# Prologue tiles taken in pairs, gate rows in four column groups of TensorE, and two products fewer per mLSTM head

## The reference, cut to what matters

```
shift, scale, gate = split(silu(c) @ w_ada + b_ada, 3)          # c (1, 1024), w_ada (1024, 3072)
h    = x * (1 + scale) + shift                                   # x (1024 tokens, 1024)
proj = h @ w_in + b_in        # q,k,v,z of the attention | q,k,v,o,z of the mLSTM | i, f (4 + 4 columns) | merge gates
A: causal stick-breaking attention, 8 heads of 64          -> y_sb
B: mLSTM in chunks, 4 heads of 128, state C, n, m carried  -> y_ml
   per chunk:  num = w_inter * (q @ C) + s_mat @ v ;  den = w_inter * (q . n) + sum(s_mat)
               C   = decay * C + (wk * k)^T @ v ;     n   = decay * n + sum(wk * k)
   init:       C = 0, n = 0
y   = (sigmoid(g_A) * y_sb + sigmoid(g_B) * y_ml) @ w_out
out = LayerNorm(2^0.25 * x + (1 + gate) * y) * ln_g + ln_b
```

## Time and profile before

| | |
|---|---|
| median of three executions | 959.51 us |
| the profiled execution, its own time | 959.67 us |
| its span (first to last instruction) | 957.8 us |
| outside the span | 1.9 us |
| TensorE busy with matmuls | 928.8 us, 97% of the span |
| VectorE, ScalarE, GpSimd busy | 616.0, 441.2, 165.5 us |
| mean granted TensorE clock | 0.997 |

### The profile page before, as it was taken

How to read it: one execution, slowest core, us unless ns; L and a number is a source line. 1 busy time by engine, 2 the same in 40 slices (tenths; PEclk the granted TensorE clock), 3 DMA queues, 4 the chain that set the end, 5 groups by cost and what they waited for, 6 DMA issues and landing times.

```text
span 957.8 us, 12945 instructions
## 1 busy us (share of the span) xinstructions
PE 928.8 (97%) x4989; PEld 760.7 (79%) x4989; DVE 616.0 (64%) x1104; ACT 441.2 (46%) x719; POOL 165.5 (17%) x114
## 2 busy tenths in 40 slices
PE   1999999999999999999999999999999999999996
PEld 1677888888888888888888888888888888887885
DVE  4856886755976647966649867534653333345997
ACT  2454566653675544675445666525743222243100
POOL 1010132220232220322311322201100000002210
PEclk9999999999999999999999999999999999999998
DMA  8942211112201022111112111127612212215232
GB/s 221 291 110 49 66 44 34 34 35 66 78 23 45 23 55 83 40 45 34 34 44 89 43 34 34 35 55 240 211 45 66 54 45 55 88 44 186 89 132 88
DMA packets 99561, 73.96 MB, mean 77 GB/s; under 512 B 4616, under 2 KB 90760, under 8 KB 99500
## 3 DMA queue, kind: packets, MB, share of 16 engines
q1 hardware_dynamic: 94828, 58.44, 23.0%
q0 software_dynamic: 2368, 8.41, 2.7%
q10 hardware_dynamic: 2304, 6.29, 1.7%
HBM read 64.59 MB, written 8.40 MB: 76 GB/s over the span
## 4 chain that ended last, share of the span: by engine, by line
PE 92%; DMA 3%; DVE 2%; SPq 2%; issue 0%; ACT 0%; DVEq 0%; ACTq 0%
PE bank L643 49%; PE bank L621 9%; PE bank L622 9%; PE bank L623 9%; PE bank L762 4%; PE bank L750 3%; DMA a_raw<-in_w_ada 2%; PE bank L737 2%; PE bank L720 2%; PE bank L739 1%; PE bank L738 1%; SPq L461 1%; PE bank L785 1%; DVE a_acc L1355 1%; PE bank L787 1%; PE bank L774 1%
## 5 line engine op out<-in xcount | busy, mean ns | idle before, releaser
L643 PE MATMUL bank<-hH,wH 128*128 128x512 f32 x688 | 271.3, 394 | 0.6 <-DVE wL L1364 0.6
L643 PE MATMUL bank<-hL,wH 128*128 128x512 f32 x688 | 271.2, 394 | 0.0
L643 PE MATMUL bank<-hH,wL 128*128 128x512 f32 x688 | 271.1, 394 | 0.0
L581 POOL TENSOR_TENSOR ez<-ez,rem 128x512 f32<-128x512 f32 x72 | 134.4, 1879 | 394.3 <-DVE rem L1524 394.3
L1364 DVE SCALAR_TENSOR_TENSOR wL<-w_raw,wH 128x512 fp32r<-128x512 f32 x116 | 99.3, 860 | 108.9 <-ACT wH L938 107.8
L643 PEld LDWEIGHTS bank<-hH,wH 128*128 128x128 f32 x688 | 129.3, 188 | 30.1 <-DVE wL L1364 2.1
L643 PEld LDWEIGHTS bank<-hH,wL 128*128 128x128 f32 x688 | 129.3, 188 | 28.7 <-issue 2.9
L643 PEld LDWEIGHTS bank<-hL,wH 128*128 128x128 f32 x688 | 129.3, 188 | 28.5 <-issue 2.9
L938 ACT ACTIVATE wH<-w_raw 128x512 fp32r<-128x512 f32 x116 | 72.5, 627 | 104.4 <-PE bank L623 71.3
L1524 DVE TENSOR_TENSOR_SCAN rem<-rem,ones 128x512 f32<-128x512 f32 (+2 forms) x96 | 99.9, 1093 | 31.7 <-ACT rem L1038 31.7
L1026 ACT ACTIVATE ez<-bank 128x512 f32<-128x512 f32 x72 | 39.1, 597 | 100.6 <-PE bank L739 100.6
(11 more groups left out here) (247 smaller groups left out, 1508.2 us busy)
## 6 DMA issues: line engine op xcount, KB each, us to landing
w_raw<-in_w_in SPq DMA_DIRECT2D x104, 256.0 KB, 2.9
a_raw<-in_w_ada SPq DMA_DIRECT2D x16, 512.0 KB, 7.3
x_rows<-in_x SPq DMA_DIRECT2D x8, 512.0 KB, 6.4
raw<-in_w_ada POOLq DMA_DIRECT2D x8, 512.0 KB, 4.7
x_in<-in_x SPq DMA_DIRECT2D x8, 512.0 KB, 4.3
out_y<-res SPq DMA_DIRECT2D x7, 512.0 KB, 2.9
raw<-in_w_out SPq DMA_DIRECT2D x10, 256.0 KB, 4.1
m_w<-bm_scratch ACTq DMA_DIRECT2D x4, 512.0 KB, 3.7
```

What stands on the lines that cost most here:

```text
L581: g.tensor_tensor(e, e, r, ALU.mult).then_inc(a_done[h], 1)
L643: ins = t.matmul(banks(number)[half][:], w, a, start=(r == 0), stop=(r == JOB_MM // 2 - 1))
```

## The change

What it does, by part:
1. **Order of the first loads.** SyncE issues c and b_ada alone, then w_ada of tile 0, then x of tile 0; the five other parameter loads go to ScalarE's queue. The parameters are transposed in two parts.
2. **Pairs.** Tiles 2 to 7 are taken as blocks of two (`BLOCKS`): w_ada and x of a block come in rows of 1 KB, VectorE folds 128x512 at a time, and `ada_columns` and `mod_columns` do both tiles at once. w_ada has four buffers, the fourth being `next_v` and `next_g`. `turn_x` no longer waits for `mod_done`.
3. **Gate rows.** No fp32r split: the weights of i and f are kept in fp32 (`w_if`) and multiplied with `h_raw` itself, in fp32. Even and odd tiles and the two halves go to four groups of partitions of one PSUM bank (start 0, 32, 64, 96), so that there are 4 matmuls per pair of tiles, 16 in all, in place of 48. VectorE adds even and odd sums (three operations on 8x512) behind `low_h(7)` and three weight splits; ScalarE evicts half 0 and then waits for VectorE (`if_moved`) before it evicts half 1.
4. **Copies of the gate rows.** The four copies to `r_i` go to GpSimd's queue; `row_logs` waits for them.
5. **Chunks.** The first chunk leaves out q by state and copies the update into the state (no memset of it); the last leaves out the update.

The core of the diff:

```
-A_BUFS = 3
+A_BUFS = 4
+BLOCKS = [[0], [1], [2, 3], [4, 5], [6, 7]]
...
-        a_raw = pt("a_raw", [P, A_BUFS, KT, 2, P])
+        a_raw = [pt(f"a_raw{n}", [P, KT * 2 * P]) for n in range(A_BUFS - 1)] + [next_vg]
+        w_if = pt("w_if", [P, KT, 2 * NH])
...
-        pro_ps = [[y_ps[0:2 * NH, :], misc_ps[2][0:2 * NH, :]],
+        pro_ps = [[y_ps[32 * n:32 * n + 2 * NH, :] for n in range(4)],
...
+            for b, tiles in enumerate(BLOCKS):
+                cols_b = slice(tiles[0] * P, (tiles[-1] + 1) * P)
+                for number, lo, hi in ada_pieces(b):
+                    if number >= A_BUFS:
+                        sp.wait_ge(ada_used, ada_freed(number))
+                    for what in range(2):
+                        sp.dma_start(ada_piece(number, lo, hi)[:, :, what], w_ada_w[:, lo:hi, what, cols_b])\
+                            .then_inc(a_in[number % A_BUFS], 16)
+                sp.dma_start(x_rows[:, :, cols_b], x_v[:, :, cols_b]).then_inc(x_cols_in[b], 16)
+                for g in {0: range(3), 3: range(3, PRO_CHUNKS)}.get(b, ()):
+                    pro_load(g)
...
-            for q in range(4):
-                sp.dma_start(r_i[32 * q:32 * q + NH, :], r_if[0:NH, :]).then_inc(rows_in, 16)
...
+            pool.wait_ge(drained[1], 1)
+            pool.wait_ge(if_moved, 3)
+            for q in range(4):
+                pool.dma_start(r_i[32 * q:32 * q + NH, :], r_if[0:NH, :]).then_inc(rows_i_in, 16)
...
+            def gate_rows(d):
+                for n in range(2):
+                    pe.wait_ge(m_drained[n], d + 3 - n)
+                if d % 4 == 0:
+                    pe.wait_ge(wL_done, PRO_K * (d // 4) + 1)
+                for odd in range(2):
+                    for half in range(2):
+                        ins = t.matmul(pro_ps[0][2 * odd + half], w_if[:, d + odd], h_raw[:, odd, halves(half)],
+                                       start=d == 0, stop=d == KT - 2, skip_group_check=True)
...
+            turn_x(0)
             ada_columns(0)
+            turn_x(1)
+            for d in range(0, KT, 2):
+                tile_of(d, 1)
+                if d == 0:
+                    ada_columns(1)
+                tile_of(d, 2)
+                gate_rows(d)
+                if d + 2 < KT:
+                    if d:
+                        ada_columns(BLOCK_OF[d + 2])
+                    turn_x(d + 2)
+                    if not d:
+                        ada_columns(BLOCK_OF[d + 2])
+                tile_of(d + 1, 1)
+                tile_of(d + 1, 2)
+                if d + 3 < KT:
+                    turn_x(d + 3)
...
+            other_columns()
+            ada_rows(0, 0, KT)
+            mod_columns(0)
+            for g in range(3):
+                pro_split(g)
+            ada_rows(1, 0, KT // 2)
+            low_h(0)
+            ada_rows(1, KT // 2, KT)
+            ada_rows(2, 0, KT // 4)
+            mod_columns(1)
+            ada_rows(2, KT // 4, KT)
+            low_h(1)
+            mod_columns(2)
+            ada_rows(3, 0, KT // 2)
+            low_h(2)
+            ada_rows(3, KT // 2, KT)
+            low_h(3)
+            for g in range(3, PRO_CHUNKS):
+                pro_split(g)
+            mod_columns(3)
+            ada_rows(4, 0, KT // 2)
+            low_h(4)
+            ada_rows(4, KT // 2, KT)
+            low_h(5)
+            mod_columns(4)
+            low_h(6)
+            low_h(7)
             for g in range(PRO_CHUNKS, PRO_CHUNKS + 3):
                 pro_split(g)
+            dve.wait_ge(filled[1], 1)
+            dve.wait_ge(rows_zero, 5)
+            rows = [r_if[0:2 * NH, halves(half)] for half in range(2)]
+            v.tensor_copy(rows[1], pro_ps[0][1]).then_inc(if_moved, 1)
+            dve.wait_ge(if_moved, 1)
+            v.tensor_tensor(rows[1], pro_ps[0][3], rows[1], ALU.add).then_inc(if_moved, 1)
+            dve.wait_ge(drained[0], 1)
+            v.tensor_tensor(rows[0], pro_ps[0][2], rows[0], ALU.add).then_inc(if_moved, 1)
...
-                    t.matmul(misc_ps[1][:, 0:P + 1], m_ktok[:, cc], m_vtok[:, cc], start=True, stop=True)\
-                        .then_inc(m_filled[1], 1)
-                    t.matmul(misc_ps[1][:, 2 * P:3 * P + 1], m_q[:, tt], m_state[:], start=True, stop=True)\
-                        .then_inc(m_filled[1], 1)
+                    if cc < NC - 1:
+                        t.matmul(misc_ps[1][:, 0:P + 1], m_ktok[:, cc], m_vtok[:, cc], start=True, stop=True)\
+                            .then_inc(m_filled[1], 1 if cc else 2)
+                    if cc:
+                        t.matmul(misc_ps[1][:, 2 * P:3 * P + 1], m_q[:, tt], m_state[:], start=True, stop=True)\
+                            .then_inc(m_filled[1], 1 if cc < NC - 1 else 2)
```

More of the change, by code:

```diff
@@ L430, in _ @@
         def _(sp):
[L431 to L440, removed]
+            sp.dma_start(prm[ROW_C:ROW_C + KT, :], c[0].rearrange("(t p) -> t p", p=P)).then_inc(c_in, 16)
+            sp.dma_start(prm[ROW_ADA:ROW_ADA + 3 * KT, :], b_ada[0].rearrange("(t p) -> t p", p=P)).then_inc(c_in, 16)
             def load(slot, src, split):
@@ L673, in turn_x, with tile_of @@
                     ins.then_inc(m_filled[n], 1)
-            def tile_of(k, first, last):
+            def gate_rows(d):
[7 more added lines that the diff above has]
+                                       start=d == 0, stop=d == KT - 2, skip_group_check=True)
+                        if d == KT - 2 and odd:
+                            ins.then_inc(filled[half], 1)
+                if d < KT - 2:
+                    ins.then_inc(if_used, 1)
+            def tile_of(k, n):
                 pe.wait_ge(hL_done, k + 1)
+                g = PRO_K * (k // 4) + n
                 if k % 4 == 0:
[L679 to L686, removed]
+                    pe.wait_ge(wL_done, g + 1)
+                w = [z[:, pro_slot(g), k % 4] for z in (w_proH, w_proL)]
+                for half in range(2):
+                    ins = split_product(pro_ps[n][half], w, (hH[:, k, halves(half)], hL[:, k, halves(half)]), k, KT)
+                    if k == KT - 1:
+                        ins.then_inc(filled[half], 1)
             def gate_columns():
@@ L997, in _ @@
                             act.wait_ge(rows_zero, 5)
-                        bias_copy(r_if[0:2 * NH, halves(half)], half, n,
-                                  r_bias[0:2 * NH, :], pro_ps[0][half])
+                        else:
+                            act.wait_ge(if_moved, 2)
+                        rows = r_if[0:2 * NH, halves(half)]
+                        bias_copy(rows, half, n, r_bias[0:2 * NH, :], rows if half else pro_ps[0][half])
                     elif n < 4:
@@ L1391, in _, with mod_columns @@
-            for d in range(KT):
-                ada_rows(d)
-                if d:
-                    low_h(d - 1)
-                mod_columns(d)
-                if d == 0:
-                    for g in range(3):
-                        pro_split(g)
-                elif d < 4:
-                    pro_split(d + 2)
-            low_h(KT - 1)
+            def mod_columns(b):
+                dve.wait_ge(ada_done, b + 1)
+                first, tiles = BLOCKS[b][0], len(BLOCKS[b])
+                bias = cols[:, ROW_ADA:ROW_ADA + 2 * KT].rearrange("p (w d) -> p w d", w=2)[:, :, first:first + tiles]
+                v.tensor_tensor(mod[:, :, first:first + tiles],
+                                ada_ps[:, 0:2 * tiles].rearrange("p (w d) -> p w d", w=2), bias, ALU.add)\
+                    .then_inc(mod_done, 1)
```

193 lines of the change are left out of this document (109 added, 84 removed).

## The result

The changed kernel takes **952.51 us** (median; 951.53 to 953.4 over 4 runs), the kernel before 959.45 beside it: ratio 0.9928, 95% interval 0.9916 to 0.9939. The forecast was 948.8 with a range of 946.0 to 953.3. So the sign and most of the steps came out, and the gain is 6.9 us instead of 10.7. The profiled execution took 953.3 us with a span of 951.6; against the one before (957.8 of span) that is 6.2 us. In a later set of runs the same kernel took 951.76 (951.16 to 953.29, 5 runs). Nine values in all, and they lie in two clumps: five from 951.16 to 951.76, four from 953.18 to 953.4. The profiled one is of the upper clump, and the experiments show what makes it.

The account below looks back on a forecast made before the run. TensorE's stream was taken to bound the kernel (matmuls fill 97% of the span). Prologue and gate-row copies give 8.9 us, chunks 1.8, together 10.7: 959.67 to 949.0, 948.8 as median; range 946.0 to 953.3.

Parts of the forecast that it names:

- rival A: Paired loads of x and w_ada: 1 KB rows flow only like 512 B rows; 6.7 us gained in all, 952.8; chance 0.10.
- m2: Waiting point behind the prologue where TensorE needs wL, at 84.39 us before; forecast at 75.5, 8.9 earlier.
- First loads: Prologue start: w_ada third in line, issued at 1.6; first fold at 8.0 instead of 11.85, 3.9 us earlier.
- Rows of 1 KB: Prologue loads of tile pairs: 344 GB/s against 290 in 512 B rows; bounds 290 and 400.
- Gate rows in four groups: `gate_rows` in the prologue: four column groups run beside each other, 1.0 us a call; bounds 1.9 and 3.5.
- rival B: `gate_rows`: the four groups run one after another, 2.5 us more per call; 5.4 gained in all, 954.1; chance 0.06.
- Tile 2's products: Prologue, first products of the first tile pair: start at 32.7 us where they started at 37.77.
- m1: Start of the first job behind the prologue, at 70.02 us before; forecast at 61.9, including a 1.8 us wait for q's eviction.
- TensorE's clock: Prologue: tiles 0 and 1 run at 1.2 GHz under the DMA; slow turn and sums of the first pair cost 0.5 us.
- Rival D: TensorE stays at 1.2 GHz through the whole prologue, so the kernel gets slower, about 971 us; chance 0.03.
- The row chain: Behind the prologue: r_f copies end at 65.9, split ready at 75.3, TensorE needs it at 75.5; the 0.6 us wait goes.
- Rival C: GpSimd's `r_i` copies land 9 us after 68.1 and delay `row_logs`; only the chunks' 1.8 remains, 957.7; chance 0.03.

Follow-up runs that it names:

- its repetition: The changed kernel run once more, with nothing altered: 951.76 us median over 5 runs; its profiled run took 953.29.

## Why the prediction was right, and where it was not

The time lies inside the range, and that is luck in part: the range's upper end was set by rival A, which fell, and the two steps that failed below had no width of their own.

- **Chunks**, 1.8 forecast, 1.5 to 1.6 measured in the span behind m2. Right.
- **First loads**, fold at 8.0 forecast, 7.96 measured. Right by some luck: the parameters were to land "before 5" and VectorE's copies to be done by 6; TensorE waited for conv_w until 6.66 and the last copy ended at 7.93, so the fold followed the copies and not w_ada. One more load on ScalarE's queue might have cost time; no run tried it.
- **Rows of 1 KB**, 344 GB/s forecast from a line between two points (48 ns a row is 341), 348 measured; x of the pair 26.3 against 26.13. Right, and rival A fell; the run in rows of 512 B priced it at 4.1 us.
- **Gate rows in four groups**, 1.0 forecast, 1.04 measured, 1.89 in two groups against the bound of 1.9. Right; rival B fell.
- **Tile 2's products**, 32.7 against 33.27, late by the slow first stretch (32.2 to 32.6 in profiles without it). m1 without the low clock, 61.9 against 62.1 to 62.8: the wait ahead of tile 4, 1.5 forecast, was 1.85 in the changed kernel's profile and 2.87 in its repetition, whose first stretch was not slow; the one for `next_q` 1.28 instead of 1.8.
- **TensorE's clock**, 0.5 us forecast, with the sentence that from 32.7 on the gaps are like those before, where the clock stayed up. This step failed. Its premise was off: behind 32.7 the longest wait of the kernel before was 0.97 us, and the changed one has 1.85 and 2.87 ahead of tile 4 in its two profiles. The low stretch at tile 4 costs 1.5 us in the executions that have it, and nothing in the others; the profiled one has it. Rival D had the mechanism, but through the whole prologue and with 971 us. The forecast's own case for the slow clock, the products at 26 us of the kernel before, rests on their step of 0.43 us alone: the granted clock reads 1.00 from 26 to 28 there.
- **The row chain**: "four issues at 0.62 and 2.29 behind the last" was to end at 65.9, TensorE to find wL ready at 75.5. This is the other step that failed. The 2.29 came from a trace in which all eight copies were on one queue. With half of them on GpSimd's it is 4.76, and wL is 1.7 late for TensorE. The working also counted one issue interval too many (the 2.29 starts with the fourth issue), 0.5 the other way. Rival C had named this place, with 9 us and a chance of 0.03, but another mechanism: GpSimd's own copies late. They landed 2.0 us behind their issue; it was SyncE's that came 2.5 late, and the kernel lost 1.8 to it.

The longest wait of TensorE behind 32.7 us in the kernel before:

```profile
41.78 0.61 PE L659 MATMUL bank<-ones,a_acc 128*128 128x1 f32 x4 [0.97 <-DVE a_acc L1358]
```

The account of m2: 75.5 forecast, 79.73 measured, 4.2 later: 0.7 from the smaller delays ahead of m1, 1.5 from the clock, 2.0 from the landing (m2 - m1 is 15.56 where 13.6 were forecast). With 0.3 less for the chunks that leaves 6.2 of the 10.7. In the executions without the low clock at tile 4, about 951.6, the landing's 2.0 are most of what is missing.

## What to carry to other kernels

A latency read from a trace belongs to what else was in flight: when a change moves transfers to another queue, even small ones, take the landing time of the neighbours as unknown and look at who waits for them. A transfer's row length is worth a run of its own, since here 512 B against 1 KB was worth more than everything else in the change. When TensorE's waits change place, allow for a slow stretch behind a new one (1.5 us here where the path had no later wait to take it up, nothing where it had), and compare kernels by marks inside the profile (here span - m2 is 871.7 to 872.0 in all twelve profiles with the shorter chunk loop) before reading a difference of a microsecond in the medians.

## What the runs showed of the hardware that was not expected

- Four 16 KB copies between SBUF rows: landing 2.29 us behind the last issue with GpSimd's queue idle, 4.14 with four like copies on it at the same time, 4.76 when weight loads follow on their own queue as well; the weight loads without GpSimd's copies add nothing.
- The same bytes in the same order: 290 GB/s in rows of 512 B, 348 in rows of 1 KB, with the DMA engines full in both.
- Eight fp32 passes of 512 columns with 8 weight columns each: 1.04 us in four column groups, 1.89 in two.
- The granted clock fell to half after a wait of 1.85 us in one execution and held after one of 2.67 in another kernel's; the price on the path was 1.5 us each time it fell at tile 4, and nothing when it fell at 28 us, ahead of a wait.
